# A hybrid block on one core: where VectorE's norm, its sine products and one step of fill stand in the order

## The chip, the cores and the metric

The kernel runs as one program on one NeuronCore of a Trainium2 chip. The metric is the device time of one execution in microseconds (us). The engines are named PE (TensorE, with its weight load PEld), DVE (VectorE), ACT (ScalarE), POOL (GpSimd) and SP (SyncE, which issues most weight loads). Each engine runs its own instructions strictly in the order of the program, and waits on semaphores that the others raise.

## The reference, cut to what matters

A sequence of 512 tokens with 16 meta tokens ahead (528 columns, width 1024) goes through two equal layers, and then through a third block with a recurrent mixer and 16 experts. The change touches only the two layers. In each of them, h is the normed input, one wide projection feeds three branches (pooling, differential attention, a recurrence), and gates weigh the branches before a feed-forward part:

```python
# recurrence (heads of 64), and what follows it
S = S * w_t + (S @ a_t) b_t^T + v_t k_t^T;  y_t = S @ r_t      # as chunks of 64 tokens
y = (y - mean) * rsqrt(var + 64e-5) * lnx_w + lnx_b
y = (y + sum(r * k * r_k) * v) * (sigmoid(gl) @ g2)
# attention
q, k = rope(h @ wq), rope(h @ wk)      # x * cos + rotated(x) * sin
a = softmax(q1 k1^T / 8) - lam * softmax(q2 k2^T / 8);  o = rms_norm(a @ v) * scale
```

## The kernel before, in words

Activations stand transposed in SBUF: 128 channels by 528 columns to a tile. PSUM has eight banks; in the stages of interest the main work takes banks 0 to 5 in turn, and banks 6 and 7 belong to the fill (below). A bank is given out again when the engine that empties it has signalled.

**Weights in two parts.** A matmul of full precision is made of three faster ones, which need each weight slab as a high and a low part. SP loads a slab into one of five ring buffers (RING), ACT rounds it (HIGHR, line 291, `high_parts`), DVE or POOL subtracts the two (RINGR, line 302, `low_parts`). The call `low_parts(..., upto)` makes every low part of DVE's that is still missing below slab number `upto`, so a later call finds nothing to do when an earlier one went as far. DVE stands still in it until ACT's high part is there.

**The fill.** While the recurrence and the attention run through short dependent steps, PE fills the time between them with gate projections. `fill(n)` on PE emits n quanta of six matmuls each; every call is logged. ACT, DVE and POOL call their own `fill()` in the same sequence; it empties finished gate halves (ACT, line 552) and makes the high and low parts up to two slabs beyond what PE had taken at the end of that logged call.

**The recurrence** (`core_pe`, `core_act`, `core_dve`) goes over five column tiles j, the first of 16 columns and four of 128 (two chunks c each). For j above 0, PE makes three products X with a fill between them, DVE adds each (line 1057), and after the last X come a fill of two quanta, the products GY and FH (48 matmuls of the program each for a tile of 128; each stands twice in the trace), and for each chunk one fill quantum and the products that read and write the state. GY waits for DVE's last X; GT and FT are DVE's sums of GY and FH (lines 1062 and 1065).

**After the recurrence** (`after_pe`, `after_act`, `after_dve`), for four channel tiles n: sums over the heads, centre (DVE, line 1139), square (ACT), variance (PE), inverse root (ACT, lines 386 and 388), then on DVE scaled (line 1146), bonus (line 1149) and out (line 1153). Out multiplies by the gate product, which PE makes in PSUM. PE's gate product n = 3 takes the bank pair of gate product n = 0, so it waits for out 0; a `fill(4)` stands just ahead of it. DVE has five `fill()` calls between centre and scaled. The first slab of the attention, `qk 0`, has number 30 in layer 0, `g2` has number 28, and the slab between them is a gate slab, whose low part is POOL's.

**The attention** (`attention_pe`, `attention_act`, `attention_dve`, `attention_pool`) starts with eight tiles m of queries (0 to 3) and keys (4 to 7). For each, PE projects `qk m` and then makes the rotation product of tile m - 1, `rot m - 1`; after the last projection stand `rot 6` and `rot 7` in a row. ACT copies the projection out of PSUM into one of two buffers, `raw_qk[m % 2]` (line 1274), POOL multiplies with the cosines (line 1451), DVE multiplies `rot m` with the sines (line 1358), and adds both (`rotated m`, lines 1364 and 1368). `rot m` on PE reads raw m. Since there are two raw buffers, ACT waits before the copy of tile m for the sum of tile m - 2:

```python
if m >= 2:
    w.wait_ge(*V[l, "rotated", m - 2])
w.wait_ge(*P[l, "qk", m])
e.copy(k.tv(k.raw_qk[m % 2]), k.pv(at[l, "qk", m])).then_inc(*A.done((l, "raw", m)))
```

Then PE projects the values in five column tiles of banks 0 to 4. Banks 0 and 1 come free with sine product 6, banks 2 and 3 with sine product 7, bank 4 with the raw copy of tile 7. The scores wait for `rotated 7`.

Of the kernel before, what the change touches and what calls it, by code (L numbers as in the profile page):

```python
# [229 lines left out]
AHEAD = 3  # L230
# [556 lines left out]
def chunks(j):  # L787
    n = TILES[j][1]
    return range(max(1, n // 64)), min(n, 64)
# [28 lines left out]
def core_pe(k, e, w, l, fill):  # L818
# [5 lines left out]
    for j, (t0, n) in enumerate(TILES):  # L824
# [69 lines left out]
        for i, src in enumerate((2, 1, 0) if j else ()):  # L894
# [8 lines left out]
            banks.emptied_by(b, 2, "core_dve", key(("X", i)))  # L903
        beside(2)

# [15 lines left out]
        for q in range(4):  # L921
# [5 lines left out]
            ins = state_part(bg, 256 + 64 * q, cw, tok(k.VT), pq(1), False)  # L927
        ins.then_inc(*P.done(key("GY")))
        for q in range(4):
            state_part(bf, 64 * q, 64, u(0), tok(k.BT), q == 0)  # L930
            state_part(bf, 256 + 64 * q, 64, tok(k.BT), u(1), False)
            ins = state_part(bf, 256 + 64 * q, 64, tok(k.KT), tok(k.VT), False)
# [26 lines left out]
def core_act(k, e, w, l, fill):  # L959
    s, at = k.s, k.banks.at  # L960
# [3 lines left out]
    for j, (t0, n) in enumerate(TILES):  # L964
# [4 lines left out]
        for kind, dst in enumerate((k.VT, k.BT, k.KT)):  # L969
# [19 lines left out]
            *A.done(key("R")))  # L989
        for i in range((5 if j else 2) + nc):  # L990
            fill()
# [7 lines left out]
def core_dve(k, e, w, l, fill):  # L999
# [4 lines left out]
    for j, (t0, n) in enumerate(TILES):  # L1004
# [47 lines left out]
        for i, dst in enumerate((1, 0, 1) if j else ()):  # L1052
# [9 lines left out]
        e.tensor_tensor(k.GT[:, 0:nc, :, 0:cw], quarter("GY")[:, :, :, 0:cw],  # L1062
                        k.Rf[:, :, t0:t0 + n].rearrange("p q (c t) -> p c q t", c=nc), ADD).then_inc(*V.done(key("GT")))
        w.wait_ge(*P[key("FH")])
        e.tensor_tensor(k.FT[:, 0:nc], quarter("FH"), over(k.c("id64"), nc, 4), ADD).then_inc(*V.done(key("FT")))
# [9 lines left out]
def core_pool(k, e, w, l, fill):  # L1075
    fill()
    w.wait_ge(*k.s["lin_dve"][l, "bonus", 3])
    e.memset(k.SB[0], 0.0).then_inc(*k.s["core_pool"].done((l, "state")))
    for j in range(5):
        for i in range((8 if j else 5) + len(chunks(j)[0])):  # L1080
            fill()
# [50 lines left out]
def after_dve(k, e, w, l, fill):  # L1132
# [8 lines left out]
    for n in range(5):  # L1141
        fill()
    low_parts(k, e, w, "lo_dve", k.slabs.index["g2", l] + AHEAD)
    for n in range(4):
        w.wait_ge(*s["post_act"][l, "var", n, "rstd"])
        e.scalar_tensor_tensor(out=k.T1[:, n], in0=k.T1[:, n], scalar=k.col("rw_lnx_w", n, l), in1=k.T3[:, n], op0=MUL,
                               op1=MUL).then_inc(*post.done((l, "scaled", n)))
        w.wait_ge(*post[l, "scaled", n])
        e.scalar_tensor_tensor(out=k.T1[:, n], in0=k.T1[:, n], scalar=k.col("rw_lnx_b", n, l), in1=k.BV[:, n], op0=ADD,
                               op1=ADD).then_inc(*post.done((l, "bonus", n)))  # L1150
        w.wait_ge(*post[l, "bonus", n])
        w.wait_ge(*s["post_pe"][l, "gate", n])
        e.tensor_tensor(k.tv(k.Rf[:, n]), k.pv(at[l, "gate", n]), k.tv(k.T1[:, n]), MUL).then_inc(
            *post.done((l, "out", n)))
# [192 lines left out]
def attention_dve(k, e, w, l, fill):  # L1347
# [5 lines left out]
    e.tensor_tensor(k.lp, lc[:, 0:4:2], lc[:, 1:4:2], MUL).then_inc(*V.done((l, "lp")))  # L1353
    for m in range(8):
        low_parts(k, e, w, "lo_dve", k.slabs.index["qk", l, m] + AHEAD)
        raw, rt = k.raw_qk[m % 2], k.rot_qk[m % 2]
        w.wait_ge(*P[l, "rot", m])
        e.tensor_tensor(k.tv(rt), k.pv(at[l, "rot", m]), k.tv(k.c("sin")), MUL).then_inc(*V.done((l, "sin", m)))
        if m >= 6:
            low_parts(k, e, w, "lo_dve", k.slabs.index["qk", l, m] + AHEAD + 1)  # L1360
        w.wait_ge(*V[l, "sin", m])
# [3 lines left out]
        else:  # L1365
            for c in range(2):
                h_ = slice(64 * c, 64 * c + 64)
                ins = e.tensor_tensor(k.KZa[h_, c, m - 4], raw[h_], rt[h_], ADD)
            ins.then_inc(*V.done((l, "rotated", m)))
    for half in range(2):  # L1370
        for kh in range(2):
# [2080 lines left out]
```

## Time and profile before

| | |
|---|---|
| median of 3 runs | 2937.75 us (2936.23 to 2937.96) |
| the profiled execution | 2937.84 us, of which its span is 2936.0 us |
| PE busy | 94% of the span |
| PEld busy | 86% |
| DVE busy | 61% |
| ACT busy | 37% |
| POOL busy | 13% |
| granted clock of PE | 0.974 of 2.4 GHz in the mean |

A line of the timeline gives start, duration, engine, line of the kernel, operation, output and inputs, how many instructions are merged, and in brackets how long the engine was idle before it and what released it. L307 is the matmul helper, L302 the low parts, L291 the high parts. A release by "issue" means that nothing in the profile held the engine. Matmuls overlap, so the step from one start to the next is shorter than the duration that is printed.

### The profile page before, as it was taken

The numbers are of one execution on the slowest core, as the hardware profiler recorded it, in microseconds if no ns is written. First come the engines' busy times: TensorE is split into PE (matmuls) and PEld (weight loads), VectorE is DVE, ScalarE is ACT, GpSimd is POOL, SyncE is SP. The second block draws the span as 40 slices with busy tenths as digits, with TensorE's granted clock in tenths as the row PEclk, the third lists the DMA queues.
The fourth block names the chain that finished last, engine by engine and source line by source line (L and its number), as shares of the span: only waits on it lengthen the run. The fifth ranks groups of instructions, "written<-read, shape, count | busy, mean of one in ns | idle before, by whom it ended". The sixth has DMA issues, their size and how long they took to land. (4 is left out here: it accounts for less than half of the span.)

```text
span 2936.0 us, 57820 instructions
## 1 busy us (share of the span) xinstructions
PE 2763.2 (94%) x25223; PEld 2536.2 (86%) x25223; DVE 1788.3 (61%) x2699; ACT 1100.4 (37%) x1777; POOL 377.3 (13%) x224
## 2 busy tenths in 40 slices
PE   8999899999999999999999999999998999699994
PEld 7998799899999998988899899999885887578873
DVE  5633244554888645733344554888625986778776
ACT  6221224523333324322324533333324343366663
POOL 0210122121111100210022120111100000000001
PEclk9999999999999999999999999999999999699997
DMA  3211122165344342211122163334321212399995
GB/s 138 76 39 35 60 83 74 53 200 200 116 134 138 123 141 89 76 46 35 52 83 70 54 198 105 115 130 142 117 93 66 95 50 65 108 402 395 389 393 206
DMA packets 115350, 380.70 MB, mean 130 GB/s; under 512 B 12800, under 2 KB 13968, under 8 KB 114704
## 3 DMA queue, kind: packets, MB, share of 16 engines
q1 hardware_dynamic: 89568, 307.18, 30.8%
q10 hardware_dynamic: 17712, 41.36, 4.0%
q0 software_dynamic: 7808, 28.34, 2.6%
q8 instruction: 204, 3.34, 0.5%
q14 instruction: 58, 0.48, 0.1%
HBM read 340.69 MB, written 36.13 MB: 128 GB/s over the span
## 5 line engine op out<-in xcount | busy, mean ns | idle before, releaser
L307 PE MATMUL PS<-HR,HIGHR 128*128 128x264 f32 (+1 forms) x3008 | 858.2, 285 | 0.0
L307 PE MATMUL PS<-XR,HIGHR 128*128 128x264 f32 (+2 forms) x1792 | 565.3, 315 | 17.3 <-DVE HR L431 10.3
L307 PEld LDWEIGHTS PS<-HR,HIGHR 128*128 128x128 f32 x3008 | 572.1, 190 | 3.1
L307 PE MATMUL PS<-XR,RINGR 128*128 128x264 f32 (+1 forms) x1600 | 457.8, 286 | 0.2 <-issue 0.2
L307 PE MATMUL PS<-HH,HIGHR 128*128 128x264 f32 (+2 forms) x1504 | 436.5, 290 | 10.9 <-ACT SMALL L388 5.7
L291 ACT CAST HIGHR<-RING 128x1024 fp32r<-128x1024 f32 (+2 forms) x340 | 330.6, 977 | 271.3 <-DMA RING<-wts 108.5
L307 PE MATMUL PS<-HH,RINGR 128*128 128x264 f32 (+2 forms) x1504 | 431.6, 287 | 0.0
L302 DVE TENSOR_TENSOR RINGR<-RING,HIGHR 128x1024 fp32r<-128x1024 f32 (+2 forms) x272 | 304.2, 1122 | 192.1 <-ACT HIGHR L291 178.4
L307 PE MATMUL PS<-ARENA 64*64 64x64 f32 (+7 forms) x8632 | 380.9, 233 | 24.6 <-issue 10.8
L307 PEld LDWEIGHTS PS<-ARENA 64*64 64x64 f32 (+4 forms) x8632 | 336.8, 139 | 57.7 <-issue 20.3
L307 PEld LDWEIGHTS PS<-XR,HIGHR 128*128 128x128 f32 x1792 | 342.0, 191 | 46.1 <-issue 15.5
L307 PEld LDWEIGHTS PS<-XR,RINGR 128*128 128x128 f32 x1600 | 305.3, 191 | 0.4 <-issue 0.4
L307 PEld LDWEIGHTS PS<-HH,HIGHR 128*128 128x128 f32 x1504 | 285.1, 190 | 17.1 <-DVE HR L431 6.5
L302 POOL TENSOR_TENSOR RINGR<-RING,HIGHR 128x1024 fp32r<-128x1024 f32 x68 | 167.3, 2462 | 962.2 <-ACT HIGHR L291 962.2
L307 PEld LDWEIGHTS PS<-HH,RINGR 128*128 128x128 f32 x1504 | 285.5, 190 | 1.4
L307 PE MATMUL PS<-WR,UBR 128*128 128x256 f32 (+1 forms) x1224 | 204.0, 323 | 3.9 <-DVE UBR L2743 3.9
L307 PEld LDWEIGHTS PS<-WR,UBR 128*128 128x128 f32 x1224 | 175.8, 189 | 23.5 <-DVE UBR L2743 4.3
L2709 DVE TENSOR_TENSOR WR<-ARENA,WR 128x1024 fp32r<-128x1024 f32 x142 | 168.7, 1218 | 32.0 <-ACT WR L2700 31.7
L1721 ACT COPY ARENA<-PS 128x528 f32<-128x528 f32 (+1 forms) x88 | 52.5, 596 | 330.1 <-PE PS L307 330.1
L1779 DVE SCALAR_TENSOR_TENSOR ARENA<-ARENA,COLS 128x528 f32<-128x528 f32 (+1 forms) x176 | 172.2, 978 | 6.2
L2700 ACT CAST WR<-ARENA 128x1024 fp32r<-128x1024 f32 x142 | 142.6, 1056 | 87.5 <-DVE RING L2887 62.1
L307 PE MATMUL PS<-FL,HIGHR 128*128 128x264 f32 (+1 forms) x528 | 169.7, 321 | 0.0
(374 smaller groups left out, 4755.9 us busy)
## 6 DMA issues: line engine op xcount, KB each, us to landing
RING<-wts SPq DMA_DIRECT2D x324, 512.0 KB, 3.6
ARENA<-wmoe SPq DMA_DIRECT2D x210, 512.0 KB, 7.0
RING<-wts SPq DMA_DIRECT2D x52, 256.0 KB, 2.9
gates<-STAGE ACTq DMA_DIRECT2D x48, 264.0 KB, 4.1
ARENA<-gates ACTq DMA_DIRECT2D x48, 264.0 KB, 3.0
ys<-RING ACTq DMA_DIRECT2D x17, 512.0 KB
ys<-STAGE POOLq DMA_DIRECT2D x15, 512.0 KB, 11.3
RING<-wts SPq DMA_DIRECT2D x16, 384.0 KB, 3.0
```

Of the source, the lines that this page charges most:

```text
L291: e.copy(k.highR[:, hs, 0:n], k.ring[:, i % NRING, 0:n]).then_inc(*k.s["hi"].done(i))
L302: e.tensor_tensor(k.ringR[:, i % NRING, 0:n], k.ring[:, i % NRING, 0:n], k.highR[:, hs, 0:n].bitcast(F32), SUB).then_inc(*k.s[name].done(i))
L307: return e.matmul(out, lhsT, rhs, start=start, stop=stop, skip_group_check=True)
L1721: e.copy(k.tv(k.RW[f % 2][p][:, 2 + FIRST[l]:530], T - FIRST[l]), k.pv(at["up", l, f, p], T - FIRST[l])).then_inc(*A.done((l, "raw", f, p)))
L1779: e.scalar_tensor_tensor(out=cv[:, own], in0=r[:, T - n + q:T + q], scalar=tap(q), in1=cv[:, own], op0=MUL, op1=ADD).then_inc(*V.done((l, ...
L2700: e.copy(high, raw).then_inc(*k.s["moe_act"].done(("high", g)))
L2709: e.tensor_tensor(low, raw, high.bitcast(F32), SUB).then_inc(*k.s["moe_dve"].done(("low", g)))
```

## The change

Three edits of the order, each in both layers; no operation is added or left out.

```diff
@@ core_pe
-        beside(2)
+        beside(1 if j else 2)
...
         ins.then_inc(*P.done(key("GY")))
+        if j:
+            beside()
         for q in range(4):
             state_part(bf, 64 * q, 64, u(0), tok(k.BT), q == 0)
@@ core_act
-        for i in range((5 if j else 2) + nc):
+        for i in range((6 if j else 2) + nc):
             fill()
@@ core_dve
                         k.Rf[:, :, t0:t0 + n]...).then_inc(*V.done(key("GT")))
+        if j:
+            fill()
         w.wait_ge(*P[key("FH")])
@@ core_pool
-        for i in range((8 if j else 5) + len(chunks(j)[0])):
+        for i in range((9 if j else 5) + len(chunks(j)[0])):
@@ after_dve
     for n in range(5):
         fill()
-    low_parts(k, e, w, "lo_dve", k.slabs.index["g2", l] + AHEAD)
     for n in range(4):
         ... scaled, bonus ...
+    for n in range(4):
+        if n == 3:
+            low_parts(k, e, w, "lo_dve", k.slabs.index["g2", l] + AHEAD)
         w.wait_ge(*post[l, "bonus", n])
         w.wait_ge(*s["post_pe"][l, "gate", n])
         e.tensor_tensor(k.tv(k.Rf[:, n]), k.pv(at[l, "gate", n]), k.tv(k.T1[:, n]), MUL)...
@@ attention_dve
+    for m in range(8):
+        low_parts(k, e, w, "lo_dve", k.slabs.index["qk", l, m] + AHEAD)
+        w.wait_ge(*P[l, "rot", m])
+        e.tensor_tensor(..., k.tv(k.c("sin")), MUL).then_inc(*V.done((l, "sin", m)))
+        if m >= 6:
+            low_parts(k, e, w, "lo_dve", k.slabs.index["qk", l, m] + AHEAD + 1)
+        if m:
+            rotated(m - 1)
+    rotated(7)
```

`rotated(m)` holds the waits and sums of tile m that stood in the body of the loop before, right behind its sine product.

**DVE after the recurrence**, layer 0, from the low parts of `qk 0` and `qk 1` (L302) on. Scaled, bonus and out are L1146, L1149 and L1153 before, L1149, L1152 and L1159 in the changed kernel. Before:

```order
L302 TENSOR_TENSOR RINGR<-RING,HIGHR 128x1024 [waits s_hi] x2
L1146 SCALAR_TENSOR_TENSOR ARENA<-ARENA,COLS 128x528 [waits s_post_act]
L1149 SCALAR_TENSOR_TENSOR ARENA<-ARENA,COLS 128x528 [waits s_post_dve]
L1153 TENSOR_TENSOR ARENA<-PS,ARENA 128x528 [waits s_post_pe,s_post_dve]
L1146 SCALAR_TENSOR_TENSOR ARENA<-ARENA,COLS 128x528 [waits s_post_act]
L1149 SCALAR_TENSOR_TENSOR ARENA<-ARENA,COLS 128x528 [waits s_post_dve]
L1153 TENSOR_TENSOR ARENA<-PS,ARENA 128x528 [waits s_post_pe,s_post_dve]
L1146 SCALAR_TENSOR_TENSOR ARENA<-ARENA,COLS 128x528 [waits s_post_act]
```

Changed:

```order
L302 TENSOR_TENSOR RINGR<-RING,HIGHR 128x1024 [waits s_hi] x2
L1149 SCALAR_TENSOR_TENSOR ARENA<-ARENA,COLS 128x528 [waits s_post_act]
L1152 SCALAR_TENSOR_TENSOR ARENA<-ARENA,COLS 128x528 [waits s_post_dve]
L1149 SCALAR_TENSOR_TENSOR ARENA<-ARENA,COLS 128x528 [waits s_post_act]
L1152 SCALAR_TENSOR_TENSOR ARENA<-ARENA,COLS 128x528 [waits s_post_dve]
L1149 SCALAR_TENSOR_TENSOR ARENA<-ARENA,COLS 128x528 [waits s_post_act]
L1152 SCALAR_TENSOR_TENSOR ARENA<-ARENA,COLS 128x528 [waits s_post_dve]
L1149 SCALAR_TENSOR_TENSOR ARENA<-ARENA,COLS 128x528 [waits s_post_act]
L1152 SCALAR_TENSOR_TENSOR ARENA<-ARENA,COLS 128x528 [waits s_post_dve]
L1159 TENSOR_TENSOR ARENA<-PS,ARENA 128x528 [waits s_post_pe] x3
L1159 TENSOR_TENSOR ARENA<-PS,ARENA 128x528 [waits s_post_pe,s_post_dve]
```

Both low parts stand ahead of the norm in either kernel: one of the five `fill()` calls makes them, and `low_parts` itself has nothing left to do at its old place or its new one. What moved is out 0, from behind the first bonus to behind the fourth.

**DVE at the last tiles of queries and keys**, layer 0, from sine product 6 on. Sine product, sum of queries and sum of keys are L1358, L1364 and L1368 before, L1376, L1366 and L1370 in the changed kernel. Before:

```order
L1358 TENSOR_TENSOR ARENA<-PS,CST 128x528 [waits s_att_pe]
L302 TENSOR_TENSOR RINGR<-RING,HIGHR 128x1024 [waits s_hi]
L1368 TENSOR_TENSOR ARENA<-ARENA 64x528 [waits s_att_pool,s_att_dve]
L1368 TENSOR_TENSOR ARENA<-ARENA 64x528
L1358 TENSOR_TENSOR ARENA<-PS,CST 128x528 [waits s_att_pe]
L302 TENSOR_TENSOR RINGR<-RING,HIGHR 128x1024 [waits s_hi]
L1368 TENSOR_TENSOR ARENA<-ARENA 64x528 [waits s_att_pool,s_att_dve]
L1368 TENSOR_TENSOR ARENA<-ARENA 64x528
```

Changed:

```order
L1376 TENSOR_TENSOR ARENA<-PS,CST 128x528 [waits s_att_pe]
L302 TENSOR_TENSOR RINGR<-RING,HIGHR 128x1024 [waits s_hi]
L1370 TENSOR_TENSOR ARENA<-ARENA 64x528 [waits s_att_pool,s_att_dve]
L1370 TENSOR_TENSOR ARENA<-ARENA 64x528
L1376 TENSOR_TENSOR ARENA<-PS,CST 128x528 [waits s_att_pe]
L302 TENSOR_TENSOR RINGR<-RING,HIGHR 128x1024 [waits s_hi]
L1370 TENSOR_TENSOR ARENA<-ARENA 64x528 [waits s_att_pool,s_att_dve]
L1370 TENSOR_TENSOR ARENA<-ARENA 64x528
L1370 TENSOR_TENSOR ARENA<-ARENA 64x528 [waits s_att_pool,s_att_dve]
L1370 TENSOR_TENSOR ARENA<-ARENA 64x528
```

Behind sine product 6 and one low part stand now the two halves of sum 5, and sums 6 and 7 stand behind sine product 7.

**PE before the state products**, layer 0, first tile of 128 columns. XR, HR, HIGHR and RINGR are fill, ARENA 64x64 is GY and FH. Before:

```order
L307 MATMUL PS<-XR,HIGHR 128x264
L307 MATMUL PS<-HR,HIGHR 128x264
L307 MATMUL PS<-XR,RINGR 128x264
L307 MATMUL PS<-ARENA 64x64 [waits s_core_dve]
L307 MATMUL PS<-ARENA 64x64 x95
L307 MATMUL PS<-XR,HIGHR 128x264
L307 MATMUL PS<-HR,HIGHR 128x264
```

Changed:

```order
L307 MATMUL PS<-XR,RINGR 128x264
L307 MATMUL PS<-ARENA 64x64 [waits s_core_dve]
L307 MATMUL PS<-ARENA 64x64 x47
L307 MATMUL PS<-XR,HIGHR 128x264
L307 MATMUL PS<-HR,HIGHR 128x264
L307 MATMUL PS<-XR,RINGR 128x264
L307 MATMUL PS<-XR,HIGHR 128x264
L307 MATMUL PS<-HR,HIGHR 128x264
L307 MATMUL PS<-XR,RINGR 128x264
L307 MATMUL PS<-ARENA 64x64 x48
L307 MATMUL PS<-XR,HIGHR 128x264
```

Six of the twelve fill matmuls that stood ahead of GY stand now between GY and FH, and the wait for DVE stands six matmuls earlier.

## Rows read from the trace of the kernel before

**Rows 1.** the page: busy us, share of span, instructions per engine

```profile
PE 2763.2 (94%) x25223; PEld 2536.2 (86%) x25223; DVE 1788.3 (61%) x2699; ACT 1100.4 (37%) x1777; POOL 377.3 (13%) x224
```

**Rows 2.** waits of PE over the span: total us, times, longest

```profile
PE PS L307 <- issue: 15.8, 13, 4.8
...
PE PS L307 <- DVE ARENA L1153: 10.2, 2, 5.1
...
PE PS L307 <- DVE ARENA L1358: 3.7, 2, 1.8
```

**Rows 3.** timeline of DVE, layer 0: start, us, operation, idle before, releaser

```profile
354.34 2.36 DVE L302 TENSOR_TENSOR RINGR<-RING,HIGHR 128x1024 fp32r<-128x1024 f32 x2 [21.31 <-ACT HIGHR L291]
356.62 0.76 DVE L1146 SCALAR_TENSOR_TENSOR ARENA<-ARENA,COLS 128x528 f32<-128x528 f32 x1
357.41 0.77 DVE L1149 SCALAR_TENSOR_TENSOR ARENA<-ARENA,COLS 128x528 f32<-128x528 f32 x1
358.21 0.71 DVE L1153 TENSOR_TENSOR ARENA<-PS,ARENA 128x528 f32<-128x528 f32 x1
```

**Rows 4.** timeline of ACT, same stretch

```profile
353.26 1.99 ACT L291 CAST HIGHR<-RING 128x1024 fp32r<-128x1024 f32 x2 [0.40 <-ACT STAGE L552]
```

**Rows 5.** timeline of PE, same stretch

```profile
358.98 2.13 PE L307 MATMUL PS<-ARENA,RING 128*128 128x264 f32 x4 [5.09 <-DVE ARENA L1153]
```

**Rows 6.** windows at that wait: busy per engine, granted clock, DMA share, GB/s

```profile
355.50:358.98 3.48, 0.00 (x1) 0.01 (x1) 3.41 (x6) 0.00 (x0) 0.00 (x0) 0.91 0.22 86
358.98:361.80 2.82, 2.82 (x9) 2.41 (x10) 2.75 (x4) 0.00 (x0) 0.00 (x0) 0.50 0.00 0
...
1465.15:1470.00 4.85, 4.85 (x18) 4.44 (x19) 4.71 (x7) 0.05 (x1) 0.00 (x0) 0.50 0.29 104
```

**Rows 7.** timeline of DVE, last tiles of queries and keys, layer 0

```profile
413.71 1.42 DVE L1368 TENSOR_TENSOR ARENA<-ARENA 64x528 f32<-64x528 f32 x2 [0.83 <-POOL ARENA L1451]
...
418.92 0.71 DVE L1358 TENSOR_TENSOR ARENA<-PS,CST 128x528 f32<-128x528 f32 x1 [2.52 <-PE PS L307]
419.54 1.89 DVE L302 TENSOR_TENSOR RINGR<-RING,HIGHR 128x1024 fp32r<-128x1024 f32 x1
421.35 2.54 DVE L1368 TENSOR_TENSOR ARENA<-ARENA 64x528 f32<-64x528 f32 x2
```

**Rows 8.** timelines of ACT and POOL, same stretch

```profile
418.08 0.60 ACT L1274 COPY ARENA<-PS 128x528 f32<-128x528 f32 x1 [5.19 <-PE PS L307]
...
419.02 3.59 POOL L1451 TENSOR_TENSOR ARENA<-ARENA,CST 128x528 f32<-128x528 f32 x2 [5.41 <-PE PS L307]
```

**Rows 9.** timeline of PE, same stretch

```profile
417.83 2.12 PE L307 MATMUL PS<-ARENA,CST 128*128 128x264 f32 x8
419.77 0.36 PE L307 MATMUL PS<-HIGHR,XR 128*128 128x256 f32 x1
...
424.69 0.39 PE L307 MATMUL PS<-HIGHR,XR 128*128 128x256 f32 x1 [1.85 <-DVE ARENA L1358]
```

**Rows 10.** timelines of PE and DVE at the state products, layer 0, tile 2

```profile
227.06 0.39 PE L307 MATMUL PS<-XR,HIGHR 128*128 128x264 f32 x1
227.29 0.29 PE L307 MATMUL PS<-HR,HIGHR 128*128 128x264 f32 x1
...
228.53 0.28 PE L307 MATMUL PS<-XR,RINGR 128*128 128x264 f32 x1
228.74 2.77 PE L307 MATMUL PS<-ARENA 64*64 64x64 f32 x170
...
227.18 1.23 DVE L1057 TENSOR_TENSOR ARENA<-PS,ARENA 128x1024 f32<-128x1024 f32 x1 [2.32 <-PE PS L307]
```

**Rows 11.** timeline of PE, idle pieces inside the state products, three tiles

```profile
232.34 0.57 PE L307 MATMUL PS<-ARENA 64*64 64x64 f32 x22 [0.83 <-issue]
...
318.12 1.35 PE L307 MATMUL PS<-ARENA 64*64 64x64 f32 x39 [3.72 <-issue]
...
1387.18 0.45 PE L307 MATMUL PS<-ARENA 64*64 64x64 f32 x12 [1.66 <-issue]
```

More of the change, by code:

```diff
@@ L1353, in attention_dve, with rotated @@
     e.tensor_tensor(k.lp, lc[:, 0:4:2], lc[:, 1:4:2], MUL).then_inc(*V.done((l, "lp")))
-    for m in range(8):
-        low_parts(k, e, w, "lo_dve", k.slabs.index["qk", l, m] + AHEAD)
+    def rotated(m):
         raw, rt = k.raw_qk[m % 2], k.rot_qk[m % 2]
[L1357 to L1360, printed above, removed]
         w.wait_ge(*V[l, "sin", m])
@@ L1369, in attention_dve @@
             ins.then_inc(*V.done((l, "rotated", m)))
+    for m in range(8):
+        low_parts(k, e, w, "lo_dve", k.slabs.index["qk", l, m] + AHEAD)
+        w.wait_ge(*P[l, "rot", m])
+        e.tensor_tensor(k.tv(k.rot_qk[m % 2]), k.pv(at[l, "rot", m]), k.tv(k.c("sin")), MUL).then_inc(
+            *V.done((l, "sin", m)))
+        if m >= 6:
[3 more added lines that the diff above has]
+    rotated(7)
     for half in range(2):
```

## The prediction

> **What bounds the kernel now.** I read the busy times first. PE is busy for 94% of the span and no other engine for more than 61% [rows 1]. So the question for each edit is where PE stands still, and whether its products come earlier or later. Next I read PE's waits over the span. Of those that stand where the change is, two are of size: on DVE's line 1153 (out 0), 5.1 us in each layer, and on line 1358 (the sine product), 1.8 us in each layer. "Issue" has 15.8 us in 13 pieces [rows 2]. If the change took away both waits on DVE and did nothing else, it would bring 10.2 + 3.7 = 13.9 us, and somewhat more from the clock. Then I read the timelines around the three places, with the order of the instructions before and after beside them. The two layers run alike, so each place is worked out on layer 0 and counted twice.
>
> **Norm and low parts.** PE waits 5.09 us ahead of gate product 3, which needs out 0's bank [rows 5]. DVE makes out 0 so late because two low parts stand ahead of the norm, and these begin only at 354.34 [rows 3], since ACT makes their high parts at 353.26 for 1.99 us [rows 4]. The edit's title says that the norm goes ahead of them. The order says otherwise: both L302 are still ahead of the first scaled, because one of the five calls of fill makes them (slabs 30 and 31), and the call that was moved had nothing left to make. So nothing starts before 356.62, as now. What does change is that out 0 now stands behind four scaled and four bonus instead of one of each. From scaled to bonus it is 357.41 - 356.62 = 0.79 us, since bonus waits for scaled. From a bonus to the next instruction that doesn't wait for it I take 0.69 us, between its 0.77 us and the 0.08 us by which the first scaled overlaps the low parts (354.34 + 2.36 - 356.62) [rows 3]. The last bonus starts at 356.62 + 3 x (0.79 + 0.69) + 0.79 = 361.85, out 0 at 362.54 and not at 358.21. That is 4.33 us later, and PE has nothing between: what is ahead of gate product 3 on PE, its fill included, is done at 358.98 - 5.09 = 353.89. What is queued behind the waiting gate product on PE is all of the attention. The total of DVE's work is the same, so outs 1 to 3, the bank of qk 0 and POOL's clearing of the key buffer are not later than now. Cost: 2 x 4.33 = +8.7 us.
>
> The clock falls in this gap already. The mean of 0.91 over 355.50 to 358.98 is 0.09 / 0.5 x 3.48 = 0.63 us at the lower level of 1.2 GHz, and the 2.82 us behind the wait have 0.50 throughout; in layer 1 all of the 4.85 us behind the same wait have 0.50 [rows 6]. At half the speed that is 1.4 us lost in layer 0 and at least 2.4 us in layer 1. A wait of 9.4 us instead of 5.1 falls once as well, so I count no difference, with 1 us to either side for each layer.
>
> **Sine products ahead of the sums.** In the middle of the eight tiles nothing is lost: sum m - 1 now waits behind sine product m, so ACT's raw copy m + 1 comes later by a sine product and a sum (0.71 us and up to 1.42 us [rows 7]) and the rotation product before them, but PE has the whole projection of qk m + 2 ahead of the product that reads it. That cover was above 5 us: ACT stood idle 5.19 us ahead of its copy, waiting for a projection [rows 8]. At the end the cover is gone. The copy of tile 7 must wait for sum 5, since both use one buffer; sum 5 is now behind sine product 6 and a low part; and PE has only rot 6 and rot 7 left, then the values. Step by step: sine product 6 at 418.92 as now, the low part at 419.54, sum 5 at 421.35 [rows 7]. That keeps the 1.81 us that the low part takes beside POOL's cosine product, against 2.36 / 2 = 1.18 us for one alone [rows 3, 8]; POOL has only one of its two products then, so this is the careful value. Sum 5 has no POOL work beside it and takes 1.42 us like sum 4 (sum 6, beside POOL, took 2.54) [rows 7]: it ends at 422.77. With 0.06 us for the signal and 0.60 us of ACT the raw copy ends at 423.43 and not at 418.68. From there to the first product of the values it was 419.77 - 418.68 = 1.09 us [rows 8, 9], so that comes at 424.52. Two column tiles of the values took 424.69 - 1.85 - 419.77 = 3.07 us [rows 9], and sine product 7 is done within them. So the third column tile starts at 427.59 and not at 424.69: the wait of 1.85 us on line 1358 is gone and one of about 4.5 us on ACT's line 1274 stands earlier. That is +2.90 us a layer. Without POOL's share (0.63 us) it would be 2.3.
>
> A gap of 4.5 us is about the size after which the clock fell in layer 0 above: 353.89 to 358.35. Behind a gap of 3.72 us 39 products took 1.35 us, 35 ns each, against 2.77 / 170 = 16 ns for the same kind at full clock, so it had fallen there too [rows 10, 11]. A fall costs 1.4 or 2.4 us as above, the mean is 1.9, and I take 1.5 for each layer, for the chance that it doesn't happen. The ends are 0 and 2.9. Cost of the part: 2 x (2.9 + 1.5) = +8.8 us, between 4.6 and 11.6.
>
> **A step of fill.** Before GY there are twelve fill matmuls, from 227.06 to GY at 228.74; DVE's last X is done at 227.18 + 1.23 = 228.41, so GY never waits. With six of them ahead (0.12 us each, from 227.29 to 228.53 in ten steps) GY could start at about 228.01, but must wait for 228.47: 0.46 us in which PE does nothing [rows 10]. The six come between GY and FH, where they hide nothing, since FH doesn't need GT. One more change of kind, into the fill and out of it, costs 0.23 - 0.12 = 0.11 us and 0.21 - 0.12 = 0.09 us [rows 10]. So a tile of 128 columns costs 0.66 us. There are four in each layer, thus 8 x 0.66 = 5.3 us if nothing absorbs it. Three of the eight have an idle piece by "issue" in the second half of GY and FH, behind the place where the six go: 0.83, 3.72 and 1.66 us [rows 11]. I read these as instructions that were not there yet, at a time that PE's delay doesn't move. Then a PE that arrives 0.66 us later waits 0.66 us less, and these three tiles cost nothing. Five are left: +3.3 us. The ends are 0, if the idle pieces shrink by more, and 5.3. No wait of PE on FT or GT is seen now and none comes, as DVE has no low part in the recurrence: the gate slabs are POOL's. ACT's and POOL's additional fill calls only keep the count.
>
> The Trainium skill ("Runtime: NRT & Kernel Launch", section "Instruction fetch mechanics") says that instructions are streamed in blocks by a DMA queue of the sequencer's own, and that this is mostly hidden because instructions are dispatched more slowly than they are filled in. By that rule there would be no idle pieces to absorb anything and this part would cost 5.3 us. The trace doesn't bear the rule out here: the 3.72 us have no other releaser [rows 11].
>
> **The sum.** 8.7 + 8.8 + 3.3 = 20.8 us. The profiled execution took 2937.84 us (span 2936.0), 0.1 above the median of 2937.75, so the two are the same for this purpose: 2937.8 + 20.8 = 2958.6 us. PE bounds the layers on both sides of these places and the third block follows the second layer, so nothing gives the time back.
>
> **The rivals.**
> 1. The sine products bring what the wait on line 1358 promises, and the copy of tile 7 is not late. For it: the wait is real, 1.8 us a layer [rows 2]. Against it: the two raw buffers, and ACT's wait for sum m - 2, which the diff leaves. Time: 2937.8 + 8.7 - 3.7 + 3.3 = 2946.1 us.
> 2. The step of fill gives the instruction stream the time that it lacks, and the idle pieces vanish, with the low clock behind the largest. For it: all three stand in the densest run of small products. Against it: 0.7 us is less than two of the three pieces. The gain would be 0.83 + 3.72 + 1.66 = 6.2 us and some 1.9 us of clock, against 5.3 us paid: 2937.8 + 8.7 + 8.8 + 5.3 - 8.1 = 2952.5 us.
> 3. On the other side, not slower: the norm is ahead of the low parts after all. Then out 0 is there when PE comes, and the 5.1 us a layer go with the 1.4 and 2.4 us of clock: 2937.8 - 14.0 + 8.8 + 3.3 = 2935.9 us, which is within 0.2% of before. It decides if the fill call that makes slabs 30 and 31 comes behind the norm. Against it: the order shows both L302 ahead. With rival 1 as well it would be 2923.4 us.
> 4. The clock recovers late at each of the four gaps and nothing is absorbed: 2 x 1 and 2 x 1.4 us more of clock, and 2.0 us: 2965.4 us.
>
> **How the numbers follow.** The forecast has a chance of 0.76, rival 1 has 0.06, rival 2 0.07, rival 3 0.03 (a third of it with rival 1), rival 4 0.08. The range from 2950 to 2966 takes in the forecast, rivals 2 and 4, less the rare ends beyond, where the clock falls in neither gap of the second part; rivals 1 and 3 are left out. That is a little over 0.8. A difference of 0.2%, 5.9 us, is about what a measurement of this kernel can tell from none. Faster by more: 0.01, rivals 3 and 1 together. Within it: 0.03, rival 3 and the smallest sums of all ends. Slower by more: 0.96.
>
> **What would show it.** In the changed profile PE's wait for the out product (line 1159 there) should be 9.4 us in each layer, with DVE's two low parts still the last thing before the first scaled. PE's wait on the sine product should be gone, and a wait of 4 to 5 us on ACT's raw copy stand before rot 7, the copy starting right behind the two halves of sum 5. Eight waits of 0.4 to 0.5 us on DVE's line 1059 should stand before GY, and the idle pieces inside GY and FH should be fewer or smaller. The prediction is wrong if PE's wait for out shrinks, if rot 7 follows rot 6 without a gap, or if the pieces by "issue" change by more than 5 us in total.

## The result, and the profile after

| | before | changed |
|---|---|---|
| median | 2937.85 us (2936.23 to 2937.96, 4 runs) | 2957.24 us (2955.55 to 2958.9, 4 runs) |
| the profiled execution | 2937.84 us, span 2936.0 us | 2958.9 us, span 2957.0 us |
| granted clock, mean | 0.974 | 0.969 |

The changed kernel is slower: the ratio is 1.006, with a 95% interval from 1.0043 to 1.0076. The forecast was 2958.6 us, between 2950 and 2966.

The busy line of the changed kernel's page (busy us, share of the span, instructions):

```profile
PE 2772.6 (94%) x25223; PEld 2544.6 (86%) x25223; DVE 1788.6 (60%) x2699; ACT 1099.5 (37%) x1777; POOL 374.9 (13%) x224
```

The counts are those of [rows 1], so no work came or went. What differs is PE's waits. Those of the changed kernel over the span (total us, times, longest), of which these four stand where the change is:

```profile
PE PS L307 <- DVE ARENA L1159: 18.8, 2, 9.4
...
PE PS L307 <- issue: 11.2, 9, 4.8
PE PS L307 <- ACT ARENA L1280: 9.3, 2, 4.6
...
PE PS L307 <- DVE ARENA L1059: 3.2, 8, 0.4
```

Against [rows 2]: the wait for out grew from 5.1 to 9.4 us in each layer, the one on the sine product (3.7 us in both layers) is replaced by one of 4.6 us a layer on the raw copy, eight waits of 0.4 us on the last X are new, and the pieces by "issue" shrank by 15.8 - 11.2 = 4.6 us.

**The norm.** The timeline of DVE in the changed kernel, layer 0, from the low parts to the last out:

```profile
358.59 2.36 DVE L302 TENSOR_TENSOR RINGR<-RING,HIGHR 128x1024 fp32r<-128x1024 f32 x2 [21.33 <-ACT HIGHR L291]
360.87 0.76 DVE L1149 SCALAR_TENSOR_TENSOR ARENA<-ARENA,COLS 128x528 f32<-128x528 f32 x1
361.67 0.77 DVE L1152 SCALAR_TENSOR_TENSOR ARENA<-ARENA,COLS 128x528 f32<-128x528 f32 x1
...
366.11 0.77 DVE L1152 SCALAR_TENSOR_TENSOR ARENA<-ARENA,COLS 128x528 f32<-128x528 f32 x1
366.80 1.93 DVE L1159 TENSOR_TENSOR ARENA<-PS,ARENA 128x528 f32<-128x528 f32 x3
369.79 0.71 DVE L1159 TENSOR_TENSOR ARENA<-PS,ARENA 128x528 f32<-128x528 f32 x1 [1.06 <-PE PS L307]
```

The two low parts are still the last work before the first scaled, and DVE stood 21.33 us idle ahead of them. From the first scaled to out 0 it is now 366.80 - 360.87 = 5.93 us; before it was 358.21 - 356.62 = 1.59 us [rows 3]. The difference is 4.34 us. Out 3 waits for PE now (1.06 us), since gate product 3 had to wait for out 0.

**The sine products.** The timeline of DVE in the changed kernel at the last tiles of layer 0:

```profile
428.73 0.71 DVE L1376 TENSOR_TENSOR ARENA<-PS,CST 128x528 f32<-128x528 f32 x1 [2.77 <-PE PS L307]
429.36 1.86 DVE L302 TENSOR_TENSOR RINGR<-RING,HIGHR 128x1024 fp32r<-128x1024 f32 x1
431.14 1.41 DVE L1370 TENSOR_TENSOR ARENA<-ARENA 64x528 f32<-64x528 f32 x2
435.47 0.71 DVE L1376 TENSOR_TENSOR ARENA<-PS,CST 128x528 f32<-128x528 f32 x1 [2.91 <-PE PS L307]
```

The timelines of ACT and then PE in the same stretch:

```profile
432.59 0.60 ACT L1280 COPY ARENA<-PS 128x528 f32<-128x528 f32 x1 [6.30 <-DVE ARENA L1370]
```

```profile
427.64 1.05 PE L307 MATMUL PS<-ARENA,CST 128*128 128x264 f32 x4
433.33 2.10 PE L307 MATMUL PS<-ARENA,CST 128*128 128x264 f32 x4 [4.64 <-ACT ARENA L1280]
434.86 0.79 PE L307 MATMUL PS<-HIGHR,XR 128*128 128x256 f32 x1
```

Read them as a chain: sine product 6 at 428.73, a low part, both halves of sum 5 at 431.14, the raw copy of tile 7 at 432.59, rot 7 at 433.33. In [rows 9] rot 6 and rot 7 are one run of eight; here they are four and four with 4.64 us between. Rot 7's four take twice as long as rot 6's (2.10 against 1.05 us): the clock has fallen. The windows of the changed kernel right behind the out wait of layer 0 and behind the raw-copy waits of layers 0 and 1 (the number before the DMA share is the granted clock):

```profile
367.56:371.00 3.44, 3.44 (x11) 3.03 (x12) 2.13 (x12) 0.00 (x0) 0.44 (x1) 0.50 0.12 27
433.33:436.50 3.17, 3.17 (x10) 2.76 (x11) 1.03 (x2) 1.75 (x2) 0.92 (x1) 0.50 0.02 5
1550.43:1554.00 3.57, 3.57 (x13) 3.20 (x14) 1.68 (x2) 1.75 (x2) 1.32 (x1) 0.54 0.00 0
```

**Where the 21.0 us between the two spans lie.** I cut each trace at starts of DVE's instructions: the first masked product of tile 0 and of tile 1 (the mask product is line 1019 before), the first centre, sine product 0, and the first copy of the values (line 1376 before). For example, layer 0's first centre starts at 329.73 before and at 333.96 in the changed kernel. The changes from before to after, in us:

| stretch | layer 0 | layer 1 |
|---|---|---|
| tile 0 of the recurrence (16 columns) | +4.48 | 0.00 |
| tiles 1 to 4 | -0.70 | +1.54 |
| first centre to sine product 0 (the norm) | +5.58 | +3.25 |
| sine product 0 to the first value copy | +4.69 | +2.61 |

That makes -0.70 + 1.54 = +0.84 for the recurrence, +8.83 for the norm and +7.30 for the sine part, 16.97 in all. The 4.48 us at tile 0 are not the change's: the two programs are the same there. PE's waits there are the same (0.4 us on ACT in both). The granted clock differs, in a window of before and then in the same one of the changed kernel:

```profile
136.00:140.00 4.00, 3.99 (x43) 3.60 (x43) 0.28 (x1) 2.01 (x4) 1.78 (x1) 1.00 0.17 68
```

```profile
136.00:140.00 4.00, 3.99 (x25) 3.68 (x22) 0.00 (x0) 2.19 (x4) 1.34 (x1) 0.70 0.17 68
```

The rest of the span (ahead of tile 0, between the layers, the third block) adds 0.45 + 0.14 - 1.07 = -0.48 us.

### The profile page after: what moved, and what is told of

It is laid out like the page before. It is cut to its first block and busy times, and to the rows that moved or that the text cites. A ratio compares the mean times of both kernels' runs of the same rounds, so it can differ in the third digit from the quotient of the medians.

```text
span 2957.0 us, 57814 instructions
## 1 busy us (share of the span) xinstructions
PE 2772.6 (94%) x25223; PEld 2544.6 (86%) x25223; DVE 1788.6 (60%) x2699; ACT 1099.5 (37%) x1777; POOL 374.9 (13%) x224
## 5 line engine op out<-in xcount | busy, mean ns | idle before, releaser
L302 DVE TENSOR_TENSOR RINGR<-RING,HIGHR 128x1024 fp32r<-128x1024 f32 (+2 forms) x272 | 306.2, 1130 | 200.7 <-ACT HIGHR L291 186.6
L307 PEld LDWEIGHTS PS<-ARENA 64*64 64x64 f32 (+4 forms) x8632 | 337.2, 139 | 57.8 <-issue 15.8
L302 POOL TENSOR_TENSOR RINGR<-RING,HIGHR 128x1024 fp32r<-128x1024 f32 x68 | 167.2, 2459 | 967.0 <-ACT HIGHR L291 967.0
```

What stands on the lines that cost most here:

```text
L302: e.tensor_tensor(k.ringR[:, i % NRING, 0:n], k.ring[:, i % NRING, 0:n], k.highR[:, hs, 0:n].bitcast(F32), SUB).then_inc(*k.s[name].done(i))
L307: return e.matmul(out, lhsT, rhs, start=start, stop=stop, skip_group_check=True)
```

## The experiments

Most kernels below differ from before by a few us, and the whole time moves by as much from run to run on the chips that they ran on (before: 2932.6 to 2957.3 us). So beside the ratio I read the stretches of the table above in each trace. All of them, in us, layer 0 / layer 1, with tiles 1 to 4 of both layers summed:

| kernel | norm | sine | tiles 1 to 4 |
|---|---|---|---|
| before | 48.75 / 49.98 | 52.20 / 53.70 | 336.07 |
| changed | 54.33 / 53.23 | 56.89 / 56.31 | 336.91 |
| e1_norm_only | 54.24 / 54.27 | 52.18 / 53.72 | 334.61 |
| e2_sine_only | 50.20 / 48.70 | 56.99 / 56.29 | 335.43 |
| e3_fill_only | 48.87 / 49.75 | 52.21 / 53.71 | 335.97 |
| e4_norm_true | 42.09 / 41.88 | 53.73 / 53.73 | 336.13 |
| e5_sine_last_pair | 50.14 / 49.17 | 50.08 / 50.09 | 337.67 |
| e6_sine_low_behind | 48.82 / 48.60 | 55.13 / 55.09 | 335.07 |
| e7_fill_both | 48.80 / 50.05 | 52.22 / 53.74 | 335.36 |
| e8_best | 42.10 / 41.89 | 50.09 / 50.08 | 335.51 |
| e9_norm_out0 | 50.16 / 48.69 | 53.70 / 52.22 | 336.14 |
| e10_sine_middle | 50.23 / 49.84 | 53.71 / 53.74 | 336.70 |
| e11_best_fill | 42.07 / 41.87 | 50.09 / 50.08 | 335.26 |

A norm stretch with before's path (e9 counted) has 16 values between 48.60 and 50.23, mean 49.42. Its mean granted clock is 0.965 in the ones below 49 us and 0.932 in the others. A sine stretch without the change's edit, or with only its middle part (e10), has one of two values, 52.2 with a granted clock of 1.00 or 53.7 with 0.97; the 14 of before, e1, e3, e4, e7, e9 and e10 have a mean of 53.18.

**Each edit alone.** e1_norm_only takes only the norm's edit:

```diff
     for n in range(5):
         fill()
-    low_parts(k, e, w, "lo_dve", k.slabs.index["g2", l] + AHEAD)
     for n in range(4):
         ... scaled, bonus ...
+    for n in range(4):
+        if n == 3:
+            low_parts(k, e, w, "lo_dve", k.slabs.index["g2", l] + AHEAD)
         ... out ...
```

> The kernel before with the first edit alone: the norm's four out products behind all four scaled and bonus, the two other edits left out. My theory: both low parts stay ahead of the norm and out 0 comes 4.33 us later, so PE's wait for it is 9.4 us in each layer and the time rises by 8.7 us, to about 2946.5 us (2944 to 2949 with the clock behind the waits). Rival: the low parts do go behind the norm, as the edit is named; then PE's wait of 5.1 us in each layer goes, and the time falls to about 2924 us.

Measured: 2952.6 us against 2941.04 for before, ratio 1.0035 (1.0017 to 1.0053). PE's wait for out (line 1155 here):

```profile
PE PS L307 <- DVE ARENA L1155: 18.8, 2, 9.4
```

The wait is that of the changed kernel, and the norm's mean over it and the changed kernel is 54.02 us, 4.60 above the 49.42: +9.2 us for both layers.

e2_sine_only takes only the sine edit:

```diff
     for m in range(8):
         low_parts(...)
         ... sine product m ...
         if m >= 6:
             low_parts(...)
-        ... sum m ...
+        if m:
+            rotated(m - 1)
+    rotated(7)
```

> The kernel before with the second edit alone: sum m - 1 behind sine product m for all eight tiles. My theory: ACT's raw copy of tile 7 waits for sum 5, PE waits some 4.6 us for that copy ahead of rot 7 in each layer, the wait of 1.8 us on the sine product goes, and a fall of the clock comes on top: +5.8 us without the clock, +7.3 us as in the trace of the change, thus 2943.7 to 2946.5 us. Rival: the wait on the sine product goes and no other comes: 2937.8 - 3.7 = 2934.1 us.

Measured: 2952.73 us, ratio 1.0037 (1.0019 to 1.0055). Its waits:

```profile
PE PS L307 <- DVE ARENA L1153: 10.2, 2, 5.1
PE PS L307 <- ACT ARENA L1274: 9.3, 2, 4.6
```

The out wait is before's, the sine product's is gone, the raw copy's is there. The sine stretch is 56.62 us in the mean of its two layers and the changed kernel's, 3.44 above 53.18: +6.9 us.

e3_fill_only takes only the fill edit, on PE (with the added `fill()` of the other engines):

```diff
-        beside(2)
+        beside(1 if j else 2)
         ... GY ...
+        if j:
+            beside()
         ... FH ...
```

> The kernel before with the third edit alone: one of the two fill steps ahead of GY stands between GY and FH. My theory as predicted: eight waits of 0.4 us for DVE's last X and two changes of kind at each, 5.3 us, less what the idle pieces by issue take up: +3.3 us, 2941.1 us. By the two traces at hand, where the recurrences of both layers together grew by 0.9 us: 2938.7 us. Rival: the step of fill gives the instructions time to arrive, the idle pieces vanish, and the time falls below 2936 us.

Measured: 2945.93 us, ratio 1.0018 (1.0002 to 1.0034).

```profile
PE PS L307 <- issue: 10.9, 9, 4.8
...
PE PS L307 <- DVE ARENA L1059: 3.2, 8, 0.4
```

Its tiles 1 to 4 take 335.97 us. The mean over the three kernels with this edit (changed, e3, e11) is 336.05 and over the nine with before's fill 335.93 (lowest 334.61, highest 337.67): +0.1 us, where the nine alone spread over 3 us. The ratio says 0.6 us or more and the stretches say nothing; the edit is worth a few us at most, and its own sign isn't settled by this pair.

The three stretch results give 9.2 + 6.9 + 0.1 = 16.2 us, or 0.55%, against the 0.6% measured. The three ratios sum to 0.90%, each with about 0.18% to either side (the root of the sum of squares is 0.31%), so they agree with 0.6% only at their edge. In us the three medians rise by 11.6, 11.7 and 4.9, 28.1 in all, where the stretches give 16.2 and the change itself 19.4 (2957.24 - 2937.85). Each of the three is above the time that was expected for it. The traces are of executions near the short end of their twelve (2946.74, 2945.83 and 2939.87 us against medians of 2952.6, 2952.73 and 2945.93). So 2 to 5 us of each pair aren't placed by any trace, and the stretches are the better measure of what an edit does at its own place.

**Norm really ahead.** e4_norm_true is e1 with the fifth `fill()` moved as well, to just ahead of the moved `low_parts`:

```diff
-    for n in range(5):
+    for n in range(4):
         fill()
...
+        if n == 3:
+            fill()
+            low_parts(k, e, w, "lo_dve", k.slabs.index["g2", l] + AHEAD)
```

> The kernel before, but with the norm and out 0 to 2 really ahead of the two low parts: DVE makes four of its five fill calls before the norm and the fifth, which makes both low parts, behind out 2. My theory: PE's wait of 5.1 us for out 0 goes in each layer and the low clock behind it (1.4 and at least 2.4 us) too: 2937.8 - 14 = 2924 us, and the low parts are no later than before since they wait for ACT. Rival: the low parts or high parts of the first query slabs become the next wait and take back half of it: about 2931 us.

Measured: 2926.54 us against 2941.04, ratio 0.9947 (0.9926 to 0.9968). The timeline of DVE in e4, layer 0:

```profile
341.11 0.77 DVE L1145 SCALAR_TENSOR_TENSOR ARENA<-ARENA,COLS 128x528 f32<-128x528 f32 x1 [5.07 <-ACT ARENA L388]
...
352.27 0.71 DVE L1156 TENSOR_TENSOR ARENA<-PS,ARENA 128x528 f32<-128x528 f32 x1 [5.14 <-PE PS L307]
...
357.38 2.36 DVE L302 TENSOR_TENSOR RINGR<-RING,HIGHR 128x1024 fp32r<-128x1024 f32 x2 [2.62 <-ACT HIGHR L291]
```

The first scaled starts as soon as ACT's root is there, at 341.11, and out 0 waits for PE and not the other way round. PE's row for gate product 3 in e4 has no idle time in front, and the windows ahead of it and from it on are at full clock:

```profile
356.77 1.05 PE L307 MATMUL PS<-ARENA,RING 128*128 128x264 f32 x4
```

```profile
351.18:356.77 5.59, 5.59 (x38) 5.20 (x37) 2.12 (x3) 0.86 (x2) 0.00 (x0) 1.00 0.09 11
356.77:360.00 3.23, 3.23 (x26) 3.10 (x25) 2.62 (x3) 1.93 (x3) 0.00 (x0) 1.00 0.96 282
```

The norm takes 41.98 us in the mean of e4, e8 and e11, 7.44 below 49.42: -14.9 us. The one call that was left in place is the difference between +9.2 and -14.9.

**Is it the place of out 0?** e9_norm_out0 keeps the edit's two loops but puts out 0 back behind bonus 0:

```diff
     for n in range(4):
         ... scaled, bonus ...
+        if n == 0:
+            out(0)
+    for n in range(1, 4):
+        out(n)
```

> The kernel before with out 0 left behind the first bonus, and only outs 1 to 3 moved behind all scaled and bonus. If the 4.33 us of out 0 are the whole cost of the first edit, this costs nothing: PE's wait for out 0 is 5.1 us as before, and the stretch from the first centre to sine product 0 is 49.4 us in the mean of the layers as before, not 54.0. Rival: outs 1 to 3, the memset on POOL and the bank of the first query product matter too; then it is above 51 us.

Measured in one execution: 2942.16 us beside 2942.47 for before.

```profile
PE PS L307 <- DVE ARENA L1145: 10.2, 2, 5.1
...
PE PS L307 <- DVE ARENA L1365: 3.7, 2, 1.9
```

Line 1145 is out here and line 1365 the sine product. The wait for out is before's again, and so is the stretch (50.16 and 48.69 us). By this one trace the place of out 0 is the whole cost of the edit; the late outs 1 to 3 cost nothing that shows.

**Which part of the sine edit costs.** e5_sine_last_pair moves only sine product 7, ahead of sum 6 and the last low part; sum 5 stays ahead of sine product 6:

```diff
         ... sine product m ...
+        if m < 6:
+            rotated(m)
+    low_parts(k, e, w, "lo_dve", k.slabs.index["qk", l, 7] + AHEAD + 1)
+    rotated(6)
+    rotated(7)
```

> The kernel before with the sums of tiles 0 to 5 in their old place, but sine product 7 right behind sine product 6, and the low parts and sums 6 and 7 behind both. Sum 5 stays ahead of sine product 6, so by my theory the raw copy of tile 7 is as early as before, rot 7 follows rot 6 without a gap, sine product 7 is done before the first column tile of the values is, and the 1.8 us in each layer go: 2937.8 - 3.7 = 2934.1 us, the stretch from sine product 0 to the first value copy 51.1 us in place of 52.9 in the mean of the layers. Rival: the wait moves to another signal (the low part of the second value slab, now later) and the time stays at 2937.8 us.

Measured: 2934.04 us against 2943.0, ratio 0.9977 (0.9959 to 0.9995). The timeline of DVE in e5, layer 0:

```profile
426.04 0.71 DVE L1370 TENSOR_TENSOR ARENA<-PS,CST 128x528 f32<-128x528 f32 x1 [2.52 <-PE PS L307]
426.67 1.88 DVE L302 TENSOR_TENSOR RINGR<-RING,HIGHR 128x1024 fp32r<-128x1024 f32 x1
428.47 0.69 DVE L1370 TENSOR_TENSOR ARENA<-PS,CST 128x528 f32<-128x528 f32 x1
```

The two sine products stand 2.43 us apart, PE has no wait on either or on the raw copy, and the stretch is 50.08 us in both layers, 3.1 below 53.18: -6.2 us for both. I had expected 51.1 us and -3.7 us: the wait goes, and with it the low clock behind it (the granted clock of the whole stretch is 1.00 in both layers), which I hadn't counted.

e6_sine_low_behind is the changed order with the low part put behind sum 5:

```diff
         ... sine product m ...
+        if m:
+            rotated(m - 1)
         if m >= 6:
             low_parts(k, e, w, "lo_dve", k.slabs.index["qk", l, m] + AHEAD + 1)
```

> The second edit alone, with the additional low part of tiles 6 and 7 behind the sum and not ahead of it. If ACT's wait for sum 5 is the cause, PE's wait ahead of rot 7 shrinks from 4.6 us by what the low part took, 1.2 to 1.8 us, less what sum 5 loses beside POOL's cosine product: 2.8 to 3.6 us, and the stretch from sine product 0 to the first value copy is 54.0 to 55.0 us in place of 56.6. Rival: the wait stays at 4.6 us, since POOL or the high parts on ACT set it.

Measured in one execution: 2942.18 us.

```profile
PE PS L307 <- ACT ARENA L1274: 7.0, 2, 3.5
```

The wait is 1.1 us shorter than e2's 4.6 and the stretch 55.1 us instead of 56.6. I had expected a stretch of 54 to 55. The low part is part of the cost; sum 5 behind sine product 6 is the larger part and remains. Sum 5 took 2.06 us here, beside POOL's products, against 1.41 us behind the low part.

e10_sine_middle keeps the changed order for tiles 1 to 5 and returns to before's from sum 5 on:

```diff
+        if 1 <= m <= 5:
+            rotated(m - 1)
+        if m >= 5:
+            rotated(m)
```

> The second edit for the first six tiles only: sums 0 to 3 behind the next sine product, sum 5 back in its old place ahead of sine product 6. If the cost is that of the end alone, nothing changes: no wait on ACT's raw copy, PE's wait of 1.8 us on sine product 7 in each layer as before, and the stretch from sine product 0 to the first value copy at 52.2 or 53.7 us as before. Rival: the raw copies that come 2 to 3 us later in the middle cost too: above 54 us.

Measured in one execution: 2947.92 us, and PE's wait on the sine product is before's, with none on the raw copy:

```profile
PE PS L307 <- DVE ARENA L1370: 3.7, 2, 1.9
```

Line 1370 is the sine product here. The stretch is 53.71 and 53.74 us, the upper of the two values that other kernels show without the edit. So the middle tiles cost nothing that can be told. The total is 5.5 us above that of before beside it (2942.47, up to 2954.95); of that the sine stretch can hold 1.1 us. The rest isn't explained; against the trace of before, tile 0 of layer 0 is 3.0 us longer and the part behind the layers 3.2 us, where neither kernel differs.

**What absorbs the wait for the last X.** e7_fill_both moves both fill quanta between GY and FH, so that PE waits longer for X:

```diff
-        beside(2)
+        beside(0 if j else 2)
         ... GY ...
+        if j:
+            beside(2)
```

> The third edit with both fill steps between GY and FH and none ahead of GY. By my theory each of the eight tiles waits 1.3 us for DVE's last X in place of 0.4, and the time ahead of idle pieces grows by as much: the recurrences of both layers together 335.6 + 10.8, less the pieces by issue that can still shrink (6.5 us are left with one step moved): 340 to 346 us. Rival: the pieces vanish wholly and the clock never falls there: below 339 us.

Measured in one execution: 2942.26 us, and 335.36 us for tiles 1 to 4. My own theory had said 340 to 346 and fell; the rival's limit of 339 held, though the pieces shrink and don't vanish wholly.

```profile
PE PS L307 <- DVE ARENA L1059: 10.6, 8, 1.3
...
PE PS L307 <- issue: 7.3, 5, 4.8
```

PE waits 10.6 us for X, and the whole is not slower. The sum hides two opposite changes: against the mean of the nine kernels with before's fill, tiles 1 to 4 take 4.0 us less in layer 0 (167.2 against 171.2) and 3.4 us more in layer 1 (168.1 against 164.7). Tile 4 of layer 0, where before has the piece of 3.72 us [rows 11], reads in e7:

```profile
318.07 1.63 PE L307 MATMUL PS<-ARENA 64*64 64x64 f32 x96 [1.33 <-DVE ARENA L1059]
321.27 1.63 PE L307 MATMUL PS<-ARENA 64*64 64x64 f32 x96
```

The piece is gone, 96 products take 1.63 us (17 ns each), and the clock holds. The windows from 318.07 to 324.00 in before and in e7:

```profile
318.07:324.00 5.93, 5.88 (x82) 5.40 (x82) 1.12 (x2) 0.00 (x0) 0.00 (x0) 0.50 0.01 3
```

```profile
318.07:324.00 5.93, 5.93 (x218) 5.51 (x219) 1.38 (x2) 1.44 (x2) 1.43 (x1) 1.00 0.37 102
```

The pieces by "issue" in the 64x64 products of both recurrences sum to 10.8 us in before (9.4 to 11.7 in the nine kernels with its fill), 6.5 in the changed kernel, 6.1 in e3, 5.8 in e11 and 2.6 in e7. Of e7's 2.6 us, 0.8 are in layer 0 and 1.8 in layer 1; of before's 10.8, 6.6 and 4.2. So layer 0 has more to give, and the largest piece with its low clock is there.

The pieces stand at fixed places of PE's program. Counted in PE's matmul records from the start of the span, every piece of layer 0, in all thirteen traces, has one of these numbers of matmuls ahead of it: 1615, 2507, 3144, 3527, 4036, 4164, 4419, 4546, 5055. Every one of layer 1 has 12763, 13782, 14675, 15312 or 15694. Within a layer these counts lie whole multiples of about 127.4 matmuls apart, each matmul with a weight load of its own. Only the fill edit changes PE's order, and only from the last X to FH, so the same count is nearly always the same instruction; it is the even distance that speaks for a cause in the stream of instructions.

**The good halves together.** e8_best joins e4 and e5; e11_best_fill adds the change's fill edit to it.

> Norm really ahead of the low parts, together with the last pair of sine products, and no fill step moved. By my theory both gains stand on their own places on PE's path and add: 2937.8 - 14.8 - 3.7 = 2919.3 us. Rival: a wait on ACT's high parts takes the place of one of them: 2924 us or more.

> The fastest version so far (norm really ahead of the low parts, last pair of sine products) together with the third edit, the moved step of fill. By the traces the moved step costs 0.9 us of the recurrences of both layers (335.6 to 336.4 us), since PE's waits for the last X are taken out of the pieces by issue: about 2920 us, not to be told from 2919. Rival, by the prediction's sum: 3.3 us more, recurrences at 339 us.

Measured: e8 2920.51 us against 2943.0, ratio 0.9942 (0.992 to 0.9965). e11 2920.2 us against 2942.47, ratio 0.9923 (0.9905 to 0.9941). Both beat before and the changed kernel. The stretches add up: 42.0 for the norm, 50.1 for the sine part, as in e4 and e5. With the fill edit the kernel isn't measurably slower than without.

## Why the prediction came out right, step by step

**The norm, +8.7 forecast.** Right in mechanism and size. Both low parts stayed ahead, out 0 came 4.34 us later where 4.33 was forecast, and PE's wait was 9.4 us as said. The mean over kernels is +9.2 us. The clock term was set at nothing, within 1 us for each layer. The pair of traces has +5.58 and +3.25, so each layer is 1.1 to 1.3 us off the 4.33, a little outside, and the two cancel. The granted clock of the whole stretch fell from 0.965 to 0.906 in layer 0 and from 0.932 to 0.904 in layer 1: before spent less time at the low level in layer 0 than in layer 1. Over all kernels the unchanged stretch moves between 48.6 and 50.2 us in this way.

**The sine products, +8.8 forecast.** The mechanism was right, one term too large. The raw copy started 432.59 - 428.73 = 3.86 us behind sine product 6, where the working had 422.83 - 418.92 = 3.91, and PE's gap was 4.64 us instead of about 4.5. The 1.78 us from the low part to sum 5 (429.36 to 431.14) confirm the careful value of 1.81. The mis-sized term is the 1.5 us of clock for each layer: the clock did fall in both, but before already pays it in part. In layer 1 of before it falls right behind the 1.85 us wait on the sine product (a row of PE's timeline and the window around it; until the wait ended the clock was full):

```profile
1532.17 0.38 PE L307 MATMUL PS<-HIGHR,XR 128*128 128x256 f32 x1 [1.85 <-DVE ARENA L1358]
```

```profile
1532.00:1535.00 3.00, 2.83 (x14) 2.83 (x15) 2.96 (x5) 0.00 (x0) 0.00 (x0) 0.59 0.00 0
```

That is the 53.7 against the 52.2 in layer 0, where the window of 3 us behind the same wait has full clock. Behind the edit both layers pay: the granted clock of the whole stretch went from 1.00 to 0.94 in layer 0 and stayed at 0.97 in layer 1. So layer 0 lost 4.69 us (2.9 and 1.8 of clock) and layer 1 only 2.61. I looked at layer 0 alone and doubled it. The measured +6.9 us lies within the forecast bounds of 4.6 to 11.6.

**The fill, +3.3 forecast.** The cost was right for what it counted: eight waits of 0.4 us (0.46 forecast). The step that failed is "Three of the eight have an idle piece ... Five are left". The prediction let a piece absorb PE's delay only in the same tile, behind the step, and at most 0.66 us of it. The runs show pieces that give way by more than the delay: the three that it named shrank by 0.83, 3.72 - 2.29 = 1.43 and 1.66 - 0.25 = 1.41 us, 3.7 us together where 2.0 were counted. The other pieces of the recurrences, among them one of 0.23 us in a fourth tile's FH (272.02, layer 0) that I had overlooked, gave 0.7 us. Together that is 10.8 - 6.5 = 4.3 us in the changed kernel, and 10.8 - 2.6 = 8.2 us in e7, where PE waits 10.6 us. The sum for the changed kernel is 3.2 us of waits and 8 x 0.2 = 1.6 us for the changes into and out of the fill (an estimate from [rows 10]), less 4.3: +0.5, with +0.84 in the pair of traces and +0.1 in the means. It is near the lower end of the forecast's 0 to 5.3. What fits is that the pieces are the price of a stream of instructions that lags behind a dense run, and that a pause ahead lets it catch up. The fixed distances between the pieces fit instructions that arrive in blocks. The trace has no record of the stream itself, so this is inferred from the pieces, their places and the waits. The rule in the Trainium skill ("Runtime: NRT & Kernel Launch", section "Instruction fetch mechanics") that fetching is mostly hidden would leave these runs no pieces to shrink, and they do shrink.

**The sum.** The forecast terms make 20.8 us, the pair of spans 21.0 us. The agreement is closer than the terms deserve: what the recurrence and the sine part fell short by (0.84 for 3.3, 7.30 for 8.8) was made up by 4.48 us of clock at tile 0 of layer 0, which no edit touches. That part was luck. Over the kernels the edits are worth 16.2 us, which would be 2954.0 us, inside the range.

**The rivals.** Rival 1 (sine gain for nothing) is out for this order, but e5 shows that the gain it named can be had. Rival 2 (pieces vanish) is half there: they shrink, the largest from 3.72 to 2.29 us, and its clock stays low (0.50 over the 5.9 us behind it, as in before). Rival 3 (norm really ahead) is out for the change and true for e4: -14.9 us measured, where the prediction priced it at -14.0.

## What to carry to other kernels

When an instruction is moved ahead of a preparation step, check every call that may make the same preparation; a call that only "makes what is missing" does nothing at its new place if an earlier one already went as far. When a consumer is moved ahead of the sums that free a ring of two buffers, look at the end of the loop, where the filler that hides the late release has run out; moving only the last pair gained about what moving all of them lost. And price a stall together with the clock behind it, in every layer separately, since a kernel may already pay for the fall.

## What the runs showed of the hardware that was not expected

- A wait of 1.85 us was followed by 3 us with a mean granted clock of 0.59 in layer 1 and by full clock in layer 0, with the same instructions around it. Over all kernels without a wait on the raw copy and with this one, the stretch shows the same two values, 52.2 us (granted clock 1.00) and 53.7 us (0.97): 1.5 us.
- The same program at tile 0 (16 columns) took 33.4 to 38.2 us in the traces, without a wait that differs. The clock does: over the whole tile it was 1.00 where the tile took 33.4 to 33.7 us, 0.91 at 36.4 to 36.7 us and 0.87 at 37.8 to 38.2 us. One pair of profiles can't price an edit of a few us unless such stretches are taken out.
- PE's waits of 10.6 us in e7 cost nothing measurable over both layers. The idle pieces inside dense 64x64 products shrank from 10.8 to 2.6 us, and with the largest went the low clock behind it: 5.93 us at half the clock, about 3 us by estimate. With 1.6 us for the changes into and out of the fill that leaves about 10.6 + 1.6 - 8.2 - 3.0 = +1.0 us, within the 3 us by which the unchanged kernels differ.
- Within a layer these pieces stand whole multiples of about 127.4 matmuls (with as many weight loads) apart, in every trace.
- DVE's two-input work is slower beside POOL's: a sum of two halves took 1.41 us alone and 2.06 to 2.54 us beside POOL's products, a low part 1.22 us alone and 1.86 to 1.89 us beside them.
